# Four waits of a decoder trunk on one core: a value projection split around the scores, output weights in halves, memsets and the last gains moved

## The reference

```python
def conformer_conv(h, w_in, b_in, w_dw, b_dw, ln_g, ln_b, w_out, b_out):
    u = h @ w_in + b_in
    a, gate = jnp.split(u, 2, axis=-1)
    u = a * jax.nn.sigmoid(gate)
    u = depthwise_causal_conv(u, w_dw, 31) + b_dw
    u = jax.nn.silu(layer_norm(u, ln_g, ln_b))
    return u @ w_out + b_out

x = x + conformer_conv(rms_norm(x, a_norm), ...)
x = x + hierarchical_moe(rms_norm(x, ffn_norm[0]), ...)
kv = rms_norm(x, kv_norm) @ w_kv          # keys (rotary) and values, 3 groups, 16 heads of 64
q = rotary(rms_norm(x, b_norm) @ w_q)     # 3 groups, 16 heads of 64
for g, (window, dil) in enumerate(((128, 1), (512, 4), (2048, 16))):
    o[g], lse[g] = dilated_group_attention(q[g], k[g], v[g], dil, window // dil)
x = x + sum(softmax(lse)[g] * o[g]) @ w_o
x = x + hierarchical_moe(rms_norm(x, ffn_norm[1]), ...)
return rms_norm(x, final_norm)
```

## Time and profile before

| | us |
|---|---|
| median of 3 runs (1705.67 to 1706.22) | 1706.2 |
| the profiled execution's own time | 1705.39 |
| its span, first to last instruction | 1703.2 |
| TensorE busy in the span | 1520.8 (89%) |
| VectorE, ScalarE, GpSimd busy | 1069.7, 667.9, 385.2 |
| head loop, from one first score to the next | 73.5 |

### The profile page before, as it was taken

How to read it: one execution, slowest core, us unless ns; L and a number is a source line. 1 busy time by engine, 2 the same in 40 slices (tenths; PEclk the granted TensorE clock), 3 DMA queues, 4 the chain that set the end, 5 groups by cost and what they waited for, 6 DMA issues and landing times. The chain is left out here.

```text
span 1703.2 us, 19568 instructions
## 1 busy us (share of the span) xinstructions
PE 1520.8 (89%) x7176; PEld 1187.9 (70%) x7176; DVE 1069.7 (63%) x1318; ACT 667.9 (39%) x725; POOL 385.2 (23%) x341
## 2 busy tenths in 40 slices
PE   6889595999999984999999999999989499999991
PEld 5779274667676743888888888888877476767660
DVE  6887535755565538766757677585753665665553
ACT  4110622555555535324243232423322355555532
POOL 3100001322222213522405042240500222222220
PEclk9989795999999996999999999999999599999996
DMA  4213523588888826212112121211203768888854
GB/s 177 77 66 127 200 85 133 185 351 341 359 351 369 351 103 251 87 50 83 56 57 86 37 76 60 74 62 49 86 29 132 316 259 359 347 366 345 350 211 172
DMA packets 52337, 309.75 MB, mean 182 GB/s; under 512 B 10320, under 2 KB 16080, under 8 KB 38480
## 3 DMA queue, kind: packets, MB, share of 16 engines
q1 hardware_dynamic: 34592, 286.03, 42.6%
q0 software_dynamic: 9648, 16.80, 2.7%
q10 hardware_dynamic: 8064, 6.50, 1.2%
HBM read 299.32 MB, written 28.31 MB: 192 GB/s over the span
## 5 line engine op out<-in xcount | busy, mean ns | idle before, releaser
L1253 DVE TENSOR_TENSOR wgl<-WR,wgh 128x2048 fp32r<-128x2048 f32 x66 | 148.6, 2290 | 214.4 <-ACT wgh L793 211.5
L636 POOL TENSOR_TENSOR KQ<-rope_ab 64x512 f32<-64x512 f32 x96 | 173.2, 1804 | 384.5 <-DVE rope_ab L1337 380.9
L1573 PE MATMUL PS<-WR,SC 128*128 128x512 f32 x528 | 233.2, 594 | 3.3 <-ACT SC L830 1.3
L862 ACT ACTIVATE wh<-wraw 128x1024 fp32r<-128x1024 f32 x80 | 84.6, 1058 | 270.2 <-PE PS L1638 247.2
L1573 PEld LDWEIGHTS PS<-WR,SC 128*128 128x128 f32 x528 | 98.8, 190 | 117.2 <-issue 115.1
L1253 DVE TENSOR_TENSOR wul<-WR,wuh 128x2048 fp32r<-128x2048 f32 x66 | 148.0, 2284 | 0.2 <-ACT wuh L793 0.2
L793 ACT ACTIVATE wgh<-WR 128x2048 fp32r<-128x2048 f32 x66 | 122.4, 1904 | 61.4 <-DMA WR<-w_gate 61.4
L793 ACT ACTIVATE wuh<-WR 128x2048 fp32r<-128x2048 f32 x66 | 122.7, 1906 | 30.4 <-PE PS L1543 18.4
L1337 DVE TENSOR_TENSOR rope_ab<-PS,rope_sb 32x512 f32<-32x512 f32 x192 | 131.9, 687 | 2.6
L1318 DVE TENSOR_TENSOR wl<-wraw,wh 128x1024 fp32r<-128x1024 f32 x80 | 98.0, 1225 | 50.0 <-ACT wh L862 48.3
L1541 PE MATMUL PS<-wgh,xgh 128*128 128x512 f32 x264 | 109.4, 415 | 0.0
(11 more groups left out here) (261 smaller groups left out, 3253.4 us busy)
## 6 DMA issues: line engine op xcount, KB each, us to landing
WR<-w_gate SPq DMA_DIRECT2D x33, 2048.0 KB, 12.2
WR<-w_up SPq DMA_DIRECT2D x33, 2048.0 KB, 16.9
WR<-w_down SPq DMA_DIRECT2D x33, 2048.0 KB, 13.0
wraw<-w_qkv SPq DMA_DIRECT2D x72, 512.0 KB, 3.3
WR<-w_in SPq DMA_DIRECT2D x8, 1024.0 KB, 5.0
WO<-w_out SPq DMA_DIRECT2D x1, 4096.0 KB, 16.0
xn_dram<-HTQ SPq DMA_DIRECT2D x8, 512.0 KB, 2.7
HT<-y_dram SPq DMA_DIRECT2D x8, 512.0 KB, 6.7
```

Of the source, the lines that this page charges most:

```text
L636: nc.gpsimd.tensor_tensor(to, cos, sin, ALU.add).then_inc(rope_done, 1)
L862: nc.scalar.activation(wh[:, s, :], wraw[:, s, :], ACT.Copy).then_inc(wh_done, 1)
L1253: V.tensor_tensor(lo[:, kts, :], raw[:, kts, :], hi[:, kts, :].bitcast(F32), ALU.subtract).then_inc(done, 1)
L1573: ins = M.matmul(PS[3 + h][:, :], hidT[:, ft, :], wd[b][:, ft, h * 512:(h + 1) * 512], start=ft == 0, stop=ft == FT - 1)
```

## The change

Four edits in one. (1) TensorE: the first twelve matmuls of values(1) go ahead of scores(0), the other twelve stay where they were. (2) SP asks for w_out in two halves, the second when the convolved tiles are back; ScalarE casts four pieces ahead of the squares, two behind them and two behind the root; VectorE makes four trails ahead of the root and four in the loop. (3) GpSimd waits for the shared norm's four normalised blocks ahead of its first memset, and no longer for mixture 0's last down product and rows. (4) The gains of the final norm go to another place (the second gate buffer) and are asked for when the last gate product is done, ahead of the rows.

```diff
--- before.py
+++ after.py
@@ -334,13 +334,14 @@
         Qh = [KQ[:, 2 + h, :, :] for h in range(2)]
         Pm = [Pm2[:, h * 1920:(h + 1) * 1920] for h in range(2)]
         masks_b = masks[:, :, :].bitcast(BF16)
-        fin_g = cut(WR, 5 * 4096, D)
+        fin_g = cut(WR, 4096, D)
 
 
 
 
         x_in = [sem(f"x_in{n}") for n in range(NT)]
-        const_in, cvec_in, bout_in, wout_in = sem("const_in"), sem("cvec_in"), sem("bout_in"), sem("wout_in")
+        const_in, cvec_in, bout_in = sem("const_in"), sem("cvec_in"), sem("bout_in")
+        wout_in = [sem(f"wout_in{b}") for b in range(2)]
         norms = ("a", "f0", "kv", "f1", "out")
         half = KT // 2
         sq_done = Count(sem("sq_done"), norms, [NT] * 5)
@@ -434,9 +435,10 @@
                 sp.dma_start(w_in_sb[c % 2].rearrange("p a b c -> p (a b c)"), a["w_in"][c]).then_inc(win_in[c % 2], 16)
             sp.wait_ge(u_mm, KT)
             sp.wait_ge(taps_done, len(BY_TAPS))
-            sp.dma_start(WO[:, :, :], a["w_out"]).then_inc(wout_in, 16)
+            sp.dma_start(WO[:, 0:KT // 2, :], a["w_out"][:, 0:KT // 2, :]).then_inc(wout_in[0], 16)
 
             sp.wait_ge(conv_in[0], (len(BY_BANDS) + 1) // 2 * PH * 16)
+            sp.dma_start(WO[:, KT // 2:, :], a["w_out"][:, KT // 2:, :]).then_inc(wout_in[1], 16)
             expert_load(0, 0, 0, wg, "w_gate", wg_in)
             expert_load(0, 0, 0, wu, "w_up", wu_in)
             expert_load(0, 1, 1, wg, "w_gate", wg_in)
@@ -481,6 +483,10 @@
                 with sp.If(two > 0):
                     expert_loads(last, (1,), 2 * before + 1)
 
+                if l == 1:
+
+                    sp.wait_ge(gate_mm[1], 2 * last + two + 1)
+                    sp.dma_start(fin_g, a["final_norm"].to_broadcast([P, D])).then_inc(fin_in, 16)
                 sp.wait_ge(y_stored[l][0], (last + 1) * 16)
                 sp.wait_ge(y_stored[l][1], seconds)
                 for n in range(NT):
@@ -516,7 +522,6 @@
             sp.dma_start(rt.rearrange("p a b -> p (a b)"), a["router"][1]).then_inc(rt_in.sem, 16)
             sp.wait_ge(wo_mm, 2 * NT)
             moe_sp(1)
-            sp.dma_start(fin_g, a["final_norm"].to_broadcast([P, D])).then_inc(fin_in, 16)
             for n in range(NT):
                 sp.wait_ge(y_ready, n + 1)
                 sp.dma_start(out[0, n * P:(n + 1) * P, :], XN["out"][:, n, :]).then_inc(out_stored, 16)
@@ -609,15 +614,12 @@
 
             moe_pool(0)
 
-            pool.wait_ge(down_mm[0], E)
-            for n in range(NT):
-                pool.wait_ge(y_back[n], 32)
+            pool.wait_ge(xn_ready.sem, xn_ready.at("kv", NT))
             steps.step(nc.gpsimd.memset(Vs[:, :, :, :, :], 1.0))
             steps.step(nc.gpsimd.memset(KQ[HEAD:P, :, :, :], 0.0))
             for h in range(2):
                 steps.step(nc.gpsimd.memset(Kh[h][HEAD:HEAD + 1, :, :], 1.0))
             pool.wait_ge(x_spilled, NT * 16)
-            pool.wait_ge(xn_ready.sem, xn_ready.at("kv", NT))
             steps.step(nc.gpsimd.memset(QKh[HEAD:P, :, :, :].bitcast(F32), 0.0))
             nc.gpsimd.memset(idle[:, :], 0.0).then_inc(att_init, 1)
             with pool.Fori(0, NP_HEADS) as i:
@@ -757,18 +759,27 @@
             out_of_phases(6)
             out_of_phases(7)
 
-            act.wait_ge(wout_in, 16)
+            def wo_lead(c):
+
+                if c % (KT // 2) == 0:
+                    act.wait_ge(wout_in[2 * c // KT], 16)
+                nc.scalar.activation(WOh[:, c, :], WO[:, c, :], ACT.Copy).then_inc(lead_done.sem, 1)
+
             act.wait_ge(bout_added, NT)
-            for c in range(KT):
-                nc.scalar.activation(WOh[:, c, :], WO[:, c, :], ACT.Copy).then_inc(lead_done.sem, 1)
+            for c in range(KT // 2):
+                wo_lead(c)
 
             for c in range(KT):
                 act.wait_ge(ln_d, c + 1)
                 if c >= 2:
                     act.wait_ge(var_mm, c - 1)
                 nc.scalar.activation(lnsq[c % 2], HTQ[:, c, :], ACT.Square).then_inc(ln_sq, 1)
+            wo_lead(4)
+            wo_lead(5)
             act.wait_ge(ln_d, KT + 1)
             nc.scalar.activation(lnstd, lnstd, ACT.Sqrt).then_inc(ln_sq, 1)
+            wo_lead(6)
+            wo_lead(7)
             for c in range(KT):
                 act.wait_ge(ln_n, c + 1)
 
@@ -1075,7 +1086,7 @@
                 dve.wait_ge(lead_done.sem, lead_done.at("w_out", c + 1))
                 steps.mark(V.tensor_tensor(WOl[:, c, :], WO[:, c, :], WOh[:, c, :].bitcast(F32), ALU.subtract))
 
-            for c in range(5):
+            for c in range(KT // 2):
                 wo_trail(c)
             dve.wait_ge(var_mm, KT)
             V.tensor_scalar(lnstd, PS[5][:, :], EPS, None, ALU.add).then_inc(ln_d, 1)
@@ -1087,7 +1098,7 @@
                     V.tensor_tensor(HTQ[:, c, :], HTQ[:, c, :], lnstd, ALU.mult).then_inc(ln_n, 1)
                 if c >= 2:
 
-                    if c - 2 >= 5:
+                    if c - 2 >= KT // 2:
                         wo_trail(c - 2)
                     dve.wait_ge(silu_lead, c - 1)
                     V.tensor_tensor(HTl[:, c - 2, :], SL[:, c - 2, :], HTh[:, c - 2, :].bitcast(F32), ALU.subtract).then_inc(silu_trail, 1)
@@ -1638,20 +1649,22 @@
                         ins = M.matmul(PS[t % 2][:, :], wlk, hi[:, kt, :], start=False, stop=kt == KT - 1)
                     ins.then_inc(unit_mm, 1)
 
-                def values(g):
-
-                    pe.wait_ge(wl_done, 9 * i + (7 + g))
+                def values(g, kts=range(KT)):
+
+                    if kts[0] == 0:
+                        pe.wait_ge(wl_done, 9 * i + (7 + g))
                     if g == 0:
                         pe.wait_ge(pairs_done, i + 1)
                     if g == 2:
                         pe.wait_ge(v_done, 3 * i + 1)
                     dst = PS[2 + g % 2][:, :]
-                    for kt in range(KT):
+                    for kt in kts:
                         whk, wlk = wh[:, g, kt * P:(kt + 1) * P], wl[:, g, kt * P:(kt + 1) * P]
                         M.matmul(dst, whk, HTh[:, kt, :], start=kt == 0, stop=False)
                         M.matmul(dst, whk, HTl[:, kt, :], start=False, stop=False)
                         ins = M.matmul(dst, wlk, HTh[:, kt, :], start=False, stop=kt == KT - 1)
-                    ins.then_inc(unit_mm, 1)
+                    if kts[-1] == KT - 1:
+                        ins.then_inc(unit_mm, 1)
 
                 def turn(g):
 
@@ -1737,9 +1750,10 @@
                     ins.then_inc(pv_mm, 1)
 
                 values(0)
+                values(1, range(KT // 2))
                 scores(0)
                 turn(0)
-                values(1)
+                values(1, range(KT // 2, KT))
                 max_rows(0)
                 scores(1)
                 turn(1)
```

## The result

The changed kernel takes 1683.78 us in the median (1682.65 to 1685.61, four runs), the one before 1705.93 (1704.27 to 1706.22, four runs): the ratio is 0.9873, with an interval of 0.9856 to 0.989. That is 22.2 us, 1.3% faster; forecast were 25.9 us and 1680.3, in a range of 1676 to 1688, so the gain came out 3.7 short. A second set of runs of the same kernel, beside the later experiments, gave 1682.58 against 1706.56, 24.0 us.

The account below looks back on a forecast made before the run. Four waits one behind the other on the path (head loop, convolution's end, shared norm, final norm's weights) were taken to add: 12.2 + 6.8 + 3.4 + 3.5 = 25.9 us off the median of 1706.2, giving 1680.3 us, range 1676 to 1688.

Parts of the forecast that it names:

- Value projection: Eight-head loop: twelve matmuls fill TensorE's hole before the first scores, head period 71.95 for 73.5, 12.2 us saved.
- the cover behind it: Head loop: ScalarE's second copy ends 0.9 us before scores(1) needs it.
- Output weights: End of the convolution: tile 7's store lands sooner and fewer casts precede the squares, 6.8 us saved (5.6 to 7.6).
- the clock's return in the squares: Convolution's end: TensorE stands less before the squares, so 0 to 1.8 us come back, taken as 1.1.
- The cost of the two casts ahead of the root: Convolution's end: pieces 4 and 5 between squares and root start the root 1.3 us later than it would.
- the fourth rival: Before the root: the table switch drains after its load, root 1.4 us later, 1681.7 us; chance 3%.
- Memsets: Shared norm: with no memset beside them VectorE's normalising instructions take about 0.75 us, 3.4 us saved (2.5 to 4.5).
- Final gains: Kernel's end: VectorE no longer stands for the final norm's weights, 3.5 us saved (2.5 to 3.5).
- The sum: Whole kernel: 12.2 + 6.8 + 3.4 + 3.5 = 25.9 us saved, median 1680.3 us; chance 71%.
- a rival within the loop: Head loop: TensorE's granted clock falls to its lower level; 1739 us with a tenth of the loop; chance 3%.

Follow-up runs that it names:

- wout_alone: Kernel before plus only the output weights in halves, with the changed order of casts and trails: 1700.85 us, ratio 0.997.
- leads_in_loop: Changed kernel with ScalarE's four late output-weight casts moved from about the root into the silu loop: 1680.26 us, ratio 0.9849 to the kernel before.
- memsets_alone: Kernel before plus only GpSimd's memsets moved behind the shared norm: 1701.91 us, ratio 0.9974.
- gains_alone: Kernel before plus only the final norm's weights in the second gate buffer, asked for before the rows: 1703.31 us, ratio 0.9981.
- order_alone: Kernel before plus the output-weights edit, but with the second half asked for right behind the first: 1705.03 us, ratio 0.9992.
- values_18: Kernel before plus only the value projection's edit, with 18 of 24 matmuls ahead of the scores: 1697.79 us, ratio 0.9958.
- values_alone: Kernel before plus only the value projection's edit, 12 of 24 matmuls ahead of the scores: 1695.12 us, ratio 0.994.
- values_6: Kernel before plus only the value projection's edit, with 6 of 24 matmuls ahead of the scores: 1694.7 us, ratio 0.9941.
- values_whole: Kernel before plus only the value projection's edit, with all 24 matmuls ahead of the scores: 1710.33 us, ratio 1.0023.

## Why the prediction held, point by point

**Value projection: right in mechanism and size.** The period went to 71.96 (71.95 forecast), eight times 1.53 are the 12.2, and the cover behind it is 1.0 (0.9 forecast).

**Output weights: 6.1 for 6.8.** The stretch gained 7.5 in the second profile, but 1.4 of that lies ahead of tile 7's store, which left at 170.43 and not 171.79; from the store on, it is 6.0 in the first and 6.1 in the second. The last mean matmul came at 177.78 (177.2 forecast), the squares at 180.00 (179.9). The term that was mis-sized is the clock's return in the squares: from the first square to the instruction behind the last it was 9.0 before and is 8.5 now, so 0.5 came back and not 1.1. The granted clock of that stretch is not a constant of the kernel: TensorE's 16 variance matmuls took 9.09 in this profile and 7.7 in those of `wout_alone` and `leads_in_loop`. The cost of the two casts ahead of the root, 1.3, was right. The last cast ends at 190.48 and the table load begins at 190.49; it ends at 191.77 and the root begins at 191.78, though its input was there since 190.5. There is no room for a drain on either side of the load, and the fourth rival falls. The Trainium skill (ScalarE: Activation LUTs, What ACT_TABLE_LOAD costs) gives a load of about 1.28 us, which the trace repeats, and a drain of about 1.38 besides, which these rows, free of any other wait, do not show.

**Memsets: right, 3.4.** Each L957 takes 0.75, and the row of L968 stays at 0.74 beside them. The Trainium skill (SBUF — State Buffer, Who interferes with whom) has VectorE and GpSimd share one pair of ports under an exclusive lock; the trace agrees, in that the tile read from SBUF was held (2.96 for 0.75) and the one read from PSUM is not.

**Final gains: 3.2 for 3.5.** The 3.51 of the earlier trace rows are gone; against them stands the wait for the second block's rows, which is 1.02 and was 0.63 before (at 1682.97). It is not the gains that hold the rows up: they were asked for at 1631.7 and had landed 3.3 later, and the first rows are asked for at 1658.09. That wait has no fixed length: in the seven other profiles that have the gains behind the rows, as before, it is 0.1 to 1.1.

**What lies outside the parts: -5.1 in this profile, -4.7 in the second one** (there the four parts made 26.5, the whole 21.9). Of those 26.5, 1.4 came ahead of tile 7's store. The sum took the rest of the kernel as unchanged. It isn't: the stretch of the last norm and the router, whose code none of the kernels touches, takes one of two lengths.

| | us | kernels |
|---|---|---|
| shorter | 48.1 to 48.4 | before, memsets_alone, gains_alone, order_alone, values_18 |
| longer | 51.1 to 51.7 | after (both profiles), values_alone, values_6, values_whole, wout_alone, leads_in_loop |

Windows of it, before and after: engines' busy time (PE, PEld, VectorE, ScalarE, GpSimd), granted clock, DMA share, GB/s. The first 12 us run at 0.86 of the clock before and at 0.72 after, and so they do in all five shorter and all seven longer profiles. TensorE's 32 transposes in the stretch take 5.16 before and 6.36 after, the router's 64 small products, which fill most of the second window, 11.41 and 13.32: 3.1 of the 3.3. In both the clock is at the lower of its two levels (0.50, 1.2 GHz) by the third window (of before not shown, 0.50 too), where TensorE is mostly idle.

```profile
1309.75:1321.75 12.00, 6.66 (x39) 5.89 (x37) 10.16 (x15) 6.17 (x14) 0.67 (x3) 0.86 0.59 218
1321.75:1333.60 11.85, 11.41 (x64) 11.32 (x64) 1.85 (x60) 1.08 (x1) 1.43 (x2) 0.63 1.00 419
```

```profile
1288.90:1300.90 12.00, 7.85 (x39) 7.08 (x37) 8.95 (x13) 4.96 (x12) 0.19 (x2) 0.72 0.59 218
1300.90:1315.90 15.00, 13.32 (x64) 13.23 (x64) 3.08 (x63) 2.28 (x4) 1.91 (x4) 0.57 1.00 421
1315.90:1340.58 24.68, 4.96 (x38) 4.26 (x39) 20.03 (x83) 8.60 (x8) 6.88 (x10) 0.50 0.63 255
```

TensorE's rows of the transposes and the products, before, then after:

```profile
1315.06 5.16 PE L1404 MATMUL PS<-ident_sb,HTQ 128*128 128x128 f32 x32 [3.81 <-DVE X L1099]
1322.17 11.41 PE L1506 MATMUL PS<-SC,HT 128*128 128x20 f32 x64 [1.95 <-ACT HT L689]
```

```profile
1294.20 6.36 PE L1415 MATMUL PS<-ident_sb,HTQ 128*128 128x128 f32 x32 [3.81 <-DVE X L1110]
1302.53 13.32 PE L1517 MATMUL PS<-SC,HT 128*128 128x20 f32 x64 [1.97 <-ACT HT L691]
```

The first windows of `values_6` and `values_18`, which differ only in one number of matmuls ahead and have the longer and the shorter length:

```profile
1295.80:1307.80 12.00, 7.79 (x39) 7.02 (x37) 8.97 (x13) 5.00 (x12) 0.26 (x2) 0.72 0.59 218
```

```profile
1300.90:1312.90 12.00, 6.75 (x39) 5.98 (x37) 10.06 (x15) 6.09 (x14) 0.66 (x3) 0.86 0.58 218
```

So the length goes with no edit: the value projection's own kernels stand on both sides, and so do those of the output weights (`wout_alone` and `order_alone`). What goes with it is how long the clock stayed low in the stretch, 36 to 37 us in the shorter and 43 to 44 in the longer. That the clock's changes fall at other places of the same work when the work comes some microseconds earlier or later is the reading that is left, and two more figures fit it. In all twelve profiles the transposes begin 5.3 after the stretch does; the clock's first fall, with TensorE idle since the output product, comes 4.6 to 5.3 after the stretch's start in the shorter ones and 3.7 to 4.5 in the longer. And the output product ahead of it is 46.0 to 46.7 in the shorter, 45.3 to 45.9 in the longer, so that some of the 3.3 was gained just before it was lost. Nothing was run to set that place on purpose; each kernel was profiled once, this one twice, so whether a kernel keeps its length from run to run stays open, and the medians tell it apart poorly (`values_alone` gained 11.1 with the longer one). The prediction had the clock as a gain in the squares and as a rival within the loop, and took it as settled everywhere else: the loop ran as forecast, and the stretches where TensorE stands and starts are the ones that moved.

Mixture 0's stretch, from the first output product to its rows, was 431.3 to 434.5 in the twelve profiles, 432.8 before and 434.3 in both of the changed kernel. The clock has a hand in it: the 64 products of its router, too, take 11.3 to 11.5 in three profiles (`values_alone`, `memsets_alone`, `leads_in_loop`) and 12.8 to 13.6 in nine. But a cost of part 2 is not excluded: four of the five profiles with it have 433.3 to 434.5, all seven without it 431.4 to 432.8, and the fifth, `leads_in_loop`, 431.3. TensorE waits for nothing within the output product in any of them; whether part 2 costs 1 to 2 us behind it stays open.

## What to carry to other kernels

A small store on the critical path can cost what shares the DMA engines with it (5.7 us here, 2.6 with the load out of its way): cut the bulk load beside it so that one piece has landed before, and ask for the rest when the small one is back. Work moved ahead to fill a hole need only fill the hole; the next wait behind it sets how much more is free, and one row of the timeline (the end of the late copy against its user) gives that number. When parts touch waits that stand one behind the other, their gains add, but a forecast of 1 or 2% should allow some 3 us for a stretch in which TensorE stands and starts, as one did here without an edit of its own.

## What was not expected of the hardware

The same stretch of unchanged code took 48.1 to 48.4 or 51.1 to 51.7 us, with nothing between in twelve profiles, as TensorE's granted clock stood at its lower level for 36 to 37 us of it or for 43 to 44; its mean over the first 12 us was 0.86 or 0.72. The sixteen variance matmuls, too, took 7.7 us in two of the profiles, 9.1 to 9.5 in eight and 10.4 in two; where the code up to them is the same (the changed kernel twice, `wout_alone`, `leads_in_loop`), 7.7 or 9.1 to 9.2.
